# Small tables placed ahead of x and h, and another end of the expert stage

## What is computed

```python
def rms_norm_2(x, g):
    return x * lax.rsqrt(jnp.mean(x * x, axis=-1, keepdims=True) + EPS) * g

def expert_choice_ffn(h, w_router, w_gate, w_up, w_down):      # 16 experts, 32 tokens each
    cap = CAPACITY_FACTOR * s // N_EXPERTS
    aff = jax.nn.softmax(h @ w_router, axis=-1)
    gate, idx = lax.top_k(aff.transpose(0, 2, 1), cap)
    xe = jnp.take_along_axis(h, idx...)                         # e, cap, d
    hid = jax.nn.silu(xe @ w_gate) * (xe @ w_up)
    ye = (hid @ w_down) * gate[..., None]
    return zeros_like(h).at[idx].add(ye)

    x = x + gt2 * expert_choice_ffn(h, ...)                     # gt2: one gate per feature
return rms_norm_2(x, g_final)
```

## Time and profile before

| | us |
|---|---|
| median of three runs | 1976.02 |
| lowest and highest run | 1974.14, 1984.43 |
| the profiled execution, its own time | 1975.01 |
| its span, first to last instruction | 1973.3 |

### The profile page before, as it was taken

How to read it: one execution, slowest core, us unless ns; L and a number is a source line. 1 busy time by engine, 2 the same in 40 slices (tenths; PEclk the granted TensorE clock), 3 DMA queues, 4 the chain that set the end, 5 groups by cost and what they waited for, 6 DMA issues and landing times.

```text
span 1973.3 us, 34966 instructions
## 1 busy us (share of the span) xinstructions
PE 1643.3 (83%) x14763; PEld 1346.4 (68%) x14763; DVE 874.6 (44%) x1191; ACT 660.9 (33%) x833; POOL 160.8 (8%) x199
## 2 busy tenths in 40 slices
PE   4999999999979999997988879569797666666665
PEld 4999799978959789976975679459795222222221
DVE  3664465556545465645546469474652000000002
ACT  4535355434444445433434824213333000000000
POOL 7400000000000000000021003024101000000000
PEclk8999999999989999998988989779998777677776
DMA  5665656754617566643342224002486999999995
GB/s 177 221 227 175 186 153 183 245 211 169 216 44 247 180 182 177 186 171 115 108 128 64 86 86 126 5 9 80 140 312 251 421 421 421 421 421 421 421 421 228
DMA packets 249771, 417.02 MB, mean 211 GB/s; under 512 B 12910, under 2 KB 210977, under 8 KB 225057
## 3 DMA queue, kind: packets, MB, share of 16 engines
q1 hardware_dynamic: 247520, 410.49, 58.1%
q10 hardware_dynamic: 2113, 4.51, 0.7%
HBM read 413.91 MB, written 1.05 MB: 210 GB/s over the span
## 4 chain that ended last, share of the span: by engine, by line
issue 69%; PE 18%; DVE 6%; POOL 4%; ACT 3%; DMA 0%; DVEq 0%; POOLq 0%; SPq 0%; ACTq 0%
PE bank L1560 3%; DVE cy L1188 2%; PE bank L376 1%; PE bank L377 1%; PE bank L378 1%; PE bank L359 1%; PE bank L360 1%; PE bank L361 1%; POOL ang L775 1%; POOL ang L776 1%; ACT w_hi L239 1%; PE bank L1478 1%; DVE w_lo L246 1%; PE bank L1670 1%; PE bank L1684 0%
## 5 line engine op out<-in xcount | busy, mean ns | idle before, releaser
L246 DVE TENSOR_TENSOR w_lo<-w_raw,w_hi 128x2048 fp32r<-128x2048 f32 (+2 forms) x178 | 402.9, 2265 | 286.4 <-ACT w_hi L239 286.2
L359 PE MATMUL bank<-h_hi,w_hi 128*128 128x256 f32 x1328 | 380.3, 286 | 13.2 <-DVE h_lo L532 10.7
L239 ACT ACTIVATE w_hi<-w_raw 128x2048 fp32r<-128x2048 f32 (+2 forms) x178 | 333.3, 1876 | 145.8 <-DMA w_raw<-in_ffn_w_down_dram 61.4
L360 PE MATMUL bank<-h_lo,w_hi 128*128 128x256 f32 x1328 | 377.7, 284 | 0.0
L361 PE MATMUL bank<-h_hi,w_lo 128*128 128x256 f32 x1328 | 377.4, 284 | 0.0
L359 PEld LDWEIGHTS bank<-h_hi,w_hi 128*128 128x128 f32 x1328 | 256.7, 193 | 17.1 <-issue 13.6
L360 PEld LDWEIGHTS bank<-h_lo,w_hi 128*128 128x128 f32 x1328 | 256.7, 193 | 0.0
L361 PEld LDWEIGHTS bank<-h_hi,w_lo 128*128 128x128 f32 x1328 | 256.6, 193 | 0.0
L2183 PE MATMUL bank<-w_exp,xeT 128*32 128x256 f32 x2048 | 177.8, 487 | 91.7 <-DMA w_exp<-in_w_up_dram 46.5
L2183 PEld LDWEIGHTS bank<-w_exp,xeT 128*32 128x32 f32 x2048 | 66.7, 130 | 197.4 <-DMA w_exp<-in_w_up_dram 87.3
L2183 PE MATMUL bank<-w_exp,hT 128*32 128x256 f32 x1024 | 96.3, 514 | 57.8 <-DMA w_exp<-in_w_down_dram 57.8
(11 more groups left out here) (462 smaller groups left out, 2835.6 us busy)
## 6 DMA issues: line engine op xcount, KB each, us to landing
w_exp<-in_w_gate_dram SPq DMA_DIRECT2D x64, 1024.0 KB, 27.0
w_exp<-in_w_up_dram SPq DMA_DIRECT2D x64, 1024.0 KB, 27.0
w_exp<-in_w_down_dram SPq DMA_DIRECT2D x64, 1024.0 KB, 27.0
w_raw<-in_ffn_w_gu_dram SPq DMA_DIRECT2D x88, 512.0 KB, 4.9
w_raw<-in_w_in_dram SPq DMA_DIRECT2D x54, 512.0 KB, 4.6
w_mod<-in_w_mod_dram SPq DMA_DIRECT2D x24, 1024.0 KB, 7.7
w_raw<-in_ffn_w_down_dram SPq DMA_DIRECT2D x44, 512.0 KB, 4.2
w_raw<-in_mem_w_kv_dram SPq DMA_DIRECT2D x32, 512.0 KB, 4.7
```

The lines of the kernel that those rows point to most:

```text
L239: e.activation(whi[slot][:, 0:w], raw[slot][:, 0:w], ACT.Copy).then_inc(S["hi_ready"], 1)
L246: e.tensor_tensor(wlo[slot][:, 0:w], raw[slot][:, 0:w], whi[slot][:, 0:w].bitcast(F32), ALU.subtract).then_inc(S["lo_ready"], 1)
L359: e.matmul(dst, whi[slot][:, lo:hi_], bh[:, k, :], start=(k == 0), stop=False)
L360: e.matmul(dst, whi[slot][:, lo:hi_], bl[:, k, :], start=False, stop=False)
```

## The change

Two parts that have nothing to do with each other.

1. The small tables stand ahead of `x`, `h_hi`, `h_lo` and `xn`. These four tiles, and `ye` and `w_exp17` with them, lie 7360 bytes higher; the tables lie 32,768 bytes lower. The rings, `a_hi`, `a_lo` and all behind them stay.
2. At the end of the experts `x` is put into the four banks by identity matmuls (after expert 4's hidden rows are turned) and the groups add to it; `y` multiplies by `gt` as it evacuates, all four blocks on VectorE; ScalarE squares the banks, tokens 0 to 127 first; each half of the tokens gets its own root, its own scaling out of PSUM and its own store of 512 KB.

```diff
--- before.py
+++ after.py
@@ -129,10 +129,6 @@
     whi = [place(f"w_hi{s}", [P, CHUNK_W], F32R) for s in range(RING)]
     wlo = [place(f"w_lo{s}", [P, CHUNK_W], F32R, offset=sbuf_at[f"w_raw{s}"]) for s in range(RING)]
     side = [place(f"w_mod{s}", [P, 2, D], F32) for s in range(RING)]
-    x = place("x", [P, TT, D], F32)
-    h_hi = place("h_hi", [P, KT, SEQ], F32R)
-    h_lo = place("h_lo", [P, KT, SEQ], F32R)
-    xn = place("xn", [P, TT, D], F32)
     ident = place("ident", [P, P], F32)
     ones = place("ones", [P, P], F32)
     vcol = place("vcol", [P, 256], F32)
@@ -143,6 +139,10 @@
     swap2 = place("swap2", [ROPE_2, ROPE_2], F32)
     rope1 = place("rope1", [ROT, 2, SEQ], F32)
     rope2 = place("rope2", [ROPE_2, 2, SEQ], F32)
+    x = place("x", [P, TT, D], F32)
+    h_hi = place("h_hi", [P, KT, SEQ], F32R)
+    h_lo = place("h_lo", [P, KT, SEQ], F32R)
+    xn = place("xn", [P, TT, D], F32)
 
     a_hi = place("a_hi", [P, FT, SEQ], F32R)
     a_lo = place("a_lo", [P, FT, SEQ], F32R)
@@ -169,16 +169,18 @@
 
     bank_free = [[] for _ in range(4)]
 
-    def finish():
+    def finish(rows_done):
 
         stored = nc.alloc_semaphore("stored")
-        waits = [all_used(), dve_evacs(), act_evacs(), (S["dve_done"], dve.n), (S["pool_done"], pool.n)]
+        waits = [all_used(), dve_evacs(), act_evacs(), (S["pool_done"], pool.n)]
 
         def store(e):
+            for t_ in range(TT):
+                e.wait_ge(*rows_done[t_])
+                e.dma_start(out[0][t_ * P:(t_ + 1) * P, :], x[:, t_, :]).then_inc(stored, 16)
             for w in waits:
                 e.wait_ge(*w)
-            e.dma_start(out[0].rearrange("(t p) d -> p t d", p=P), x[:, :, :]).then_inc(stored, 16)
-            e.wait_ge(stored, 16)
+            e.wait_ge(stored, 16 * TT)
         sp.raw(store)
         with nc.Block() as block:
             for engine, queue in ((block.tensor, pe), (block.scalar, act), (block.vector, dve),
@@ -2144,9 +2146,9 @@
     done_before = [(S["pe_done"], pe.n), (S["act_done"], act.n), (S["dve_done"], dve.n), act_evacs(), dve_evacs()]
     act.do(lambda e: e.activation(small[:, 178:179], neg_half[:, 0:1], ACT.Silu))
     NCH = 12 * E
-    e_used, e_silu, e_hid, e_turned, e_hT, e_yea, e_yev, e_gates, e_out = (nc.alloc_semaphore(n_) for n_ in (
+    e_used, e_silu, e_hid, e_turned, e_hT, e_yev, e_gates, e_out = (nc.alloc_semaphore(n_) for n_ in (
         "expert_chunk_used", "expert_silu", "expert_hidden", "expert_turned", "expert_hidden_T",
-        "expert_y_act", "expert_y_dve", "gates_turned", "expert_group_out"))
+        "expert_y_dve", "gates_turned", "expert_group_out"))
     XG, XD, XT = X[0:2], X[2], X[3]
 
     chunk_at = {key: n_ for n_, key in enumerate(order())}
@@ -2195,7 +2197,6 @@
         def down(x_):
             e.wait_ge(e_hT, x_ + 1)
             if x_:
-                e.wait_ge(e_yea, x_)
                 e.wait_ge(e_yev, x_)
             else:
                 e.wait_ge(e_gates, 2)
@@ -2221,14 +2222,19 @@
                     ins = e.transpose((XD, XT)[g_ // 2][:, o_:o_ + P], SG[:, t_, g_ * P:(g_ + 1) * P], ident[:, :])
             ins.then_inc(e_gates, 1)
 
+        def residual_in():
+
+            for t_ in range(TT):
+                for hf in range(2):
+                    e.matmul(G[2 * t_ + hf][:, :], ident[:, :], x[:, t_, hf * BANK:(hf + 1) * BANK], start=True, stop=False)
+
         def group_out(g_):
 
-            e.wait_ge(e_yea, 4 * g_ + 4)
             e.wait_ge(e_yev, 4 * g_ + 4)
             for t_ in range(TT):
                 for hf in range(2):
                     e.matmul(G[2 * t_ + hf][:, :], GT[:, g_, t_ * P:(t_ + 1) * P], ye[:, g_, hf * BANK:(hf + 1) * BANK],
-                             start=(g_ == 0), stop=(g_ == E // 4 - 1)).then_inc(e_out, 1)
+                             start=False, stop=(g_ == E // 4 - 1)).then_inc(e_out, 1)
 
         for x_ in range(E):
             gate_up(x_)
@@ -2237,6 +2243,8 @@
             else:
                 down(x_ - 1)
             turn_hidden(x_)
+            if x_ == 4:
+                residual_in()
             if x_ % 4 == 1 and x_ > 4:
                 group_out(x_ // 4 - 1)
         down(E - 1)
@@ -2267,13 +2275,6 @@
             if x_ >= 2:
                 e.wait_ge(*used("w_down_2", x_ - 2, 3))
             e.activation(hT[x_ % 2][:, :, :], XT[:, 0:W4].rearrange("p (c q) -> p c q", c=2), ACT.Copy).then_inc(e_hT, 1)
-
-        def y(x_):
-            e.wait_ge(*used("w_down_2", x_, 3))
-            for c in range(2):
-                ins = e.activation(ye[32 * (x_ % 4):32 * (x_ % 4) + 32, x_ // 4, c * W4:(c + 1) * W4],
-                                   XD[32 * c:32 * c + 32, 0:W4], ACT.Copy)
-            ins.then_inc(e_yea, 1)
 
         for x_ in range(E):
             silu(x_)
@@ -2282,10 +2283,7 @@
                 for b in range(2):
                     ins = e.activation(GT[:, 2 * b:2 * b + 2, :], (XD, XT)[b][:, :].rearrange("p (g t) -> p g t", g=2), ACT.Copy)
                 ins.then_inc(e_gates, 1)
-            else:
-                y(x_ - 1)
             hidden_T(x_)
-        y(E - 1)
     act.raw(act_experts)
 
     def dve_experts(e):
@@ -2300,9 +2298,9 @@
 
         def y(x_):
             e.wait_ge(*used("w_down_2", x_, 3))
-            for c in range(2, 4):
-                ins = e.tensor_copy(ye[32 * (x_ % 4):32 * (x_ % 4) + 32, x_ // 4, c * W4:(c + 1) * W4],
-                                    XD[32 * c:32 * c + 32, 0:W4])
+            for c in range(4):
+                ins = e.tensor_tensor(ye[32 * (x_ % 4):32 * (x_ % 4) + 32, x_ // 4, c * W4:(c + 1) * W4],
+                                      XD[32 * c:32 * c + 32, 0:W4], gt[32 * c:32 * c + 32, 1, c * W4:(c + 1) * W4], ALU.mult)
             ins.then_inc(e_yev, 1)
 
         for x_ in range(E):
@@ -2312,20 +2310,29 @@
         y(E - 1)
     dve.raw(dve_experts)
 
+
     outs = E // 4 * 4
+    msq, rstd = small[:, 128:132], small[:, 136:138]
+    rows_done = []
     for t_ in range(TT):
         for hf in range(2):
-            tp = (e_out, outs - 4 + 2 * t_ + hf + 1)
             cs = slice(hf * BANK, (hf + 1) * BANK)
-            t = dve.do(lambda e, t_=t_, hf=hf, cs=cs: e.tensor_tensor(xn[:, t_, cs], G[2 * t_ + hf][:, :], gt[:, 1, cs], ALU.mult), tp)
-            t = dve.do(lambda e, t_=t_, cs=cs: e.tensor_tensor(x[:, t_, cs], x[:, t_, cs], xn[:, t_, cs], ALU.add), t)
-
-    rs, t = rstd_rows(x, [t], D)
+            t = act.do(lambda e, t_=t_, hf=hf, cs=cs: e.activation(
+                xn[:, t_, cs], G[2 * t_ + hf][:, :], ACT.Square, scale=D ** -0.5, accum_out=msq[:, 2 * t_ + hf:2 * t_ + hf + 1]),
+                (e_out, outs - 4 + 2 * t_ + hf + 1))
+        t = dve.do(lambda e, t_=t_: e.scalar_tensor_tensor(
+            out=rstd[:, t_:t_ + 1], in0=msq[:, 2 * t_:2 * t_ + 1], scalar=EPS, in1=msq[:, 2 * t_ + 1:2 * t_ + 2],
+            op0=ALU.add, op1=ALU.add), t)
+        t = pool.do(lambda e, t_=t_: e.tensor_tensor(rstd[:, t_:t_ + 1], rstd[:, t_:t_ + 1], neg_half[:, 0:1], ALU.pow), t, t_nh)
+        rows_done.append(t)
     for t_ in range(TT):
-        dve.do(lambda e, t_=t_, rs=rs: e.scalar_tensor_tensor(
-            out=x[:, t_, :], in0=x[:, t_, :], scalar=rs[:, t_:t_ + 1], in1=gf2[:, :],
-            op0=ALU.mult, op1=ALU.mult), t, (g2_in, 16))
-    return finish()
+        for hf in range(2):
+            cs = slice(hf * BANK, (hf + 1) * BANK)
+            t = dve.do(lambda e, t_=t_, hf=hf, cs=cs: e.scalar_tensor_tensor(
+                out=x[:, t_, cs], in0=G[2 * t_ + hf][:, :], scalar=rstd[:, t_:t_ + 1], in1=gf2[:, cs],
+                op0=ALU.mult, op1=ALU.mult), rows_done[t_], (g2_in, 16))
+        rows_done[t_] = t
+    return finish(rows_done)
 
 
 def constants():
```

## The result

| | before | after |
|---|---|---|
| median, lowest and highest of seven runs, us | 1976.02 (1970.34 to 1984.43) | 1955.64 (1954.77 to 1964.59) |
| the profiled execution | 1975.01 | 1955.47 |
| its span | 1973.3 | 1953.7 |

The ratio is 0.990, 95% interval 0.9879 to 0.9922: 20.4 us less by the medians, 19.5 by the profiled executions. The forecast was 1950.

A forecast was written before the change was run, and what follows sets the result against it. TensorE was taken to bound the products, DMA the experts, a chain the last 18 us. Gains of 22.0 us (tables) and 3.2 us (end), together 25.2, took the median 1976.02 to 1950.8, said as 1950; range 1940 to 1975.

The forecast's parts named there:

- The bound: Whole kernel: TensorE bounds the products up to 1500 us, DMA the experts at 421 GB/s; the last 18 us are a chain.
- the reading of the windows: Products: `h` matmuls take 120.0 ns, `a` 113.2 to 117.9; the address tells them apart, not the operand's role.
- equal remainders or not: Products: operand pairs with equal address remainders are slow, unequal ones fast; `h` would go from 120.0 to 113.3 or 117.7 ns.
- the price for one matmul: Products on `h`: each matmul at full clock gains 5.2 ns, 120.0 less `a`'s mean of 114.8.
- the count: Matmuls on `h`: 5136, less 672 in the delta rule, leaves 4464; 95% at 2.4 GHz, 4240, gain 22.0 us.
- The group: After the last chunk: the eight-instruction matmul group keeps its 6.28 us, perhaps 1.2 shorter or as much longer.
- The sign of being wrong that the forecast named: Products: pacing by VectorE once TensorE is 4% faster, its share in the windows near 20 of 20 us.
- Rival B: Products: addresses don't count, or the part of memory does; only the end gains, 1973 us; chance 0.34.
- Rival C: Products: all stretches take the slower of `a`'s two paces; 9.8 + 3.2 = 13 us gained, 1963 us; chance 0.13.
- Rival D: Delta rule: `h` gains nothing and the other 2396 matmuls lose 6.7 ns each; 1989 us; chance 0.05.
- Rival E: End of the kernel: the tail doesn't shrink, `y` and the clock eat it; worth 2 us; no chance given.
- case A: Products: the remainder counts, with mixed paces; 1950 us, from 1943 to 1957, elsewhere 1941 to 1960; chance 0.48.

The follow-up runs named there:

- the sweep: Separate kernel, nothing of the reference computed: TensorE alone runs the products' two matmul patterns at start distances 0 to 224 bytes; 113.3 to 120.0 ns from start to start.
- the halves apart: Changed kernel with each half's two scalings issued right behind its own root: median 1952.16 us, ratio 0.9879; run again, 1950.5 us, ratio 0.9864.
- the two with 64 bytes: Only `neg_half` and `eps` ahead of `x`: in the kernel before, 1964.18 us; in the changed kernel with scalings right behind each half's root, 1963.12 us.
- those with 32 and with 7296: Kernel before with only `neg_half` ahead of `x` (32 bytes), 1968.86 us; with all tables but `neg_half` and `eps` there (7296 bytes), 1974.63 us.
- the second group: The changed kernel run once more without any edit, four runs: median 1959.31 us, ratio 0.9896 to the kernel before.

## Why the prediction was right, and where it was off

- **The bound.** Right: TensorE in the products, DMA in the experts (in the 50 us from 1680 us on after the change a DMA share of 1.01 and 421 GB/s, TensorE busy for 32.98). From the first expert matmul to the last `y` it took 445.7 us before and 445.3 after (1508.99 to 1954.73, 1493.40 to 1938.73), so the four residual matmuls are hidden.
- **Part 1, the reading of the windows.** Right. `h` at 120.0 and `a` at 113 to 118 ns were two classes of address, not two sorts of tile, as lowering `a` by 64 bytes showed. Right, too, that the role alone doesn't tell them apart. Incomplete: "equal remainders or not". With a distance of 7296 bytes, also unequal modulo 8192 and 1024, `h` would have gained 1.3 ns instead of 6.7. 7360 was well chosen, because 192 is one of the two distances of the sweep that reach 113.3 ns, and the one that mostly does so with `h` moving. The forecast took it from `a_hi`; its rule alone would have allowed 7296 as well, or 64, which is 12.6 us worse.
- **Part 1, the price for one matmul.** I took 5.2 ns, the mean of `a`. Up to 1023 us stand 3888 of the 5136 matmuls on `h`, 3504 of them with `h` moving. At granted clock 1.00 these went from 119.96 to 114.3 ns, those with `h` stationary from 119.9 to 117.8: some 20.4 us by the counts (3500 x 5.6 + 384 x 2.2), 19.9 by the starts. The price holds. So does leaving out the lower clock: at 0.50 the products' matmuls in a row start 213.4 ns apart in both kernels (88 distances before, 110 after), so there the move of `h` brought nothing. That is 256 columns in 213.4 ns, or 1.20 per ns; the 1.2 GHz of the forecast stand for this and its 2.4 GHz, by the granted shares, for twice as much.
- **Part 1, the count: the term that was mis-sized.** 22.0 us were forecast, and 16.0 came. Of the 4464 counted, 3888 stand before 1023 us: at the forecast's 95% and 5.2 ns that is 19.2 us, and 19.9 came (the share at granted clock 1.00 is nearer 99%, which made up for little). The other 576 were priced at 2.8 us and gave nothing. There `h` got faster too, yet the stretches don't get shorter, since TensorE is not alone on the path (59.9 of 71 us busy, 108.1 of 146 in the delta rule's part). I had left out the delta rule for this reason, but not its neighbours. On top of that, 4.3 us of the lead were lost after 1003 us to stretches that took longer than before: 1.2 us in the first, 2.8 between the delta rule and the experts, 1.7 of them in the part whose granted clock is 0.94 instead of 0.98. The experts gave 0.4 back. How much is lost belongs to the execution: the same layout reached the experts with 20.0, 15.6, 8.1, 7.5 and 5.8 us of lead in five profiles. The forecast held a pace as mixed; it didn't hold the clock as a draw, and that is worth as much.

The clock behind the delta rule, before and after:

```profile
1323.00:1429.00 106.00, 93.13 (x1439) 88.05 (x1435) 55.18 (x67) 36.46 (x42) 32.79 (x26) 0.98 0.31 99
```

```profile
1305.00:1412.00 107.00, 94.13 (x1423) 88.71 (x1424) 55.35 (x67) 36.29 (x42) 32.24 (x26) 0.94 0.30 98
```

What differs is one stretch of 6.8 us at clock 0.50, 50.6 us behind the delta rule's end. Of the five profiles with this layout four have it, and take 188.2 to 188.6 us from there to the experts; the fifth, the halves apart again, doesn't and takes 185.2, though its program is that of a profile which has it. The three profiles with `h` unmoved don't have it (185.6 to 185.8 us), nor do the two with 64 bytes; those with 32 and with 7296 do. So it isn't a fixed price of the layout; whether the layout makes it likelier is open.

- **Part 2.** Forecast -3.15, measured -3.5. `y` +0.86 (0.87 to 1.73; forecast +0.85). The group 6.41, forecast 6.28 kept. From TensorE's end (1940.52 + 6.41 = 1946.93) to the end of the last scaling (1950.60) 3.67 us instead of 6.67: -3.0, forecast -2.8. From there to the end of the span 3.15 us instead of 4.58: -1.4, forecast -1.2. The forecast said that VectorE would have the first half's scaling queued behind the second half's sum, and it does: the root is there at 1945.84, the scaling starts at 1947.87. The sign of being wrong that the forecast named, VectorE near 20 of 20 us, did not come either: 12.6 and 16.0 us. How large part 2 looks depends a little on the execution of before: from `y` to the end six profiles with the old end take 17.9 to 18.6 us, the three with the changed one 15.0 to 15.1.
- **Rival B** (addresses don't count, or the part of the memory does; part 2 alone, 1976.0 - 3.2 = 1973) fell by the result, by the 64 and 7296 bytes and by the lowered `a`. The sweep has nothing at work on the core but TensorE, and the pace still runs from 113.3 to 120.0 ns by the distance of the two operands. Why it does, no run here shows. **Rival C** (all in the slower pace) came near in part: whole stretches, and in one profile both long ones, are at 117.8. That both long ones were at 113.3 in the first profile was in part luck. **Rival D** (1989: `h` gains nothing, and the delta rule's other 2396 matmuls, through `xn` and the tiles laid over it, lose 6.7 ns each) did not happen: the delta rule's stretch is 146.0 us before and 146.2 after. **Rival E** neither.
- **The range**, 1940 to 1975, holds the result; the changed kernel's other runs, up to 1965.64, too. For case A the forecast gives two ranges, 1943 to 1957 and 1941 to 1960; the result of 1955.64 lies in both, the second group's median of 1959.31 only in the wider.

## What to carry to other kernels

Read TensorE's pace as a distance from start to start in dense windows at full clock, for each pair of operands, and compare equal matmuls; a difference of a few per cent may be nothing but the start addresses, and one `place` line of padding can win it back. Choose the distance of moving minus stationary operand by a sweep, not by "unequal". When a gain of this size is forecast, count only the stretches in which TensorE is alone on the path, and expect the clock to give or take several us in each execution of a program like this one (here the lead at the experts was 5.8 to 20.0 us with one layout).

## What the runs showed of the hardware

- For float32r matmuls of 256 columns with a new 128 x 128 load before each, the distance from start to start at granted clock 1.00 was 120.0 ns at equal start addresses modulo 256, 118.7 at a distance of 128, 113.3 or 117.8 at 64 and 192, and 116.7 to 120.0 at odd multiples of 32, with no other engine at work; 121.2 in two of the mixed placements of the hi and lo parts. In the kernel `a` at a distance of 128 had 118.7 or 120.0. At granted clock 0.50 it was 213.4 ns with `h` at 0 and at 192.
- At distances of 64 and 192 the pace was mostly one of two fixed values, 113.3 and 117.8 ns, held over an unbroken row of up to 1054 matmuls; it could differ behind the next break and in the next execution.
- The time at granted clock 0.50 before the experts was 154 to 201 us in twelve profiles of nearly the same program, and a stretch of some 70 us took 70.4 to 80.2 us with it.
